# An attention routine that keeps its scores negated, and takes fewer small VectorE operations per unit

## The reference

```python
def diff_attention(q, k, v, lam, slopes):
    ...
        s = jnp.einsum('bhcqd,bhckd->bhcqk', qb, k).astype(jnp.float32) * scale
        s = s - slopes[None, :, None, None, None] * dist
        s = jnp.where(dist >= 0, s, -jnp.inf)
        p = jax.nn.softmax(s, axis=-1)
        p = p[:, :, 0] - lam * p[:, :, 1]
        return jnp.einsum('bhqk,bhkd->bhqd', p.astype(v.dtype), v)

def selected_attention(q, k, v, sel_idx, slopes):
    ...
        s = s - slopes[None, :, :, None, None] * dist
        s = jnp.where(dist >= 0, s, -jnp.inf)
        p = jax.nn.softmax(s, axis=-1)
        return jnp.einsum('bhgqk,bhqkd->bhgqd', p.astype(vg.dtype), vg)
```

## Time and profile before

| What | Value |
|---|---|
| Median of 3 runs | 2819.24 us (2817.35 to 2819.33) |
| The profiled execution, its own time | 2822.95 us |
| Its span in the trace | 2820.8 us |
| PE busy in the span | 2575.7 us, 91% |
| DVE busy in the span | 1466.9 us, 52% |
| ACT busy in the span | 1013.2 us, 36% |
| The three attention calls | 516 to 816 us and 848 to 992 us of the span |

### The profile page before, as it was taken

How to read it: one execution, slowest core, us unless ns; L and a number is a source line. 1 busy time by engine, 2 the same in 40 slices (tenths; PEclk the granted TensorE clock), 3 DMA queues, 4 the chain that set the end, 5 groups by cost and what they waited for, 6 DMA issues and landing times. The chain is left out here.

```text
span 2820.8 us, 34813 instructions
## 1 busy us (share of the span) xinstructions
PE 2575.7 (91%) x12876; PEld 2119.4 (75%) x12876; DVE 1466.9 (52%) x3370; ACT 1013.2 (36%) x2275; POOL 180.5 (6%) x188
## 2 busy tenths in 40 slices
PE   8999986899996679997989999889799999999998
PEld 6887865777985668885658888666578887888877
DVE  5244266855888874218874732478672323223235
ACT  4223132444674442217861232344442223122132
POOL 2000000000000011101200001343000000000000
PEclk9999986799998989999999999899799999999999
DMA  4112120000000054110011132000541111111113
GB/s 149 31 46 78 56 62 1 1 1 1 1 1 1 1 175 116 38 27 14 25 53 49 49 131 101 30 1 1 194 157 38 49 55 47 49 49 46 49 55 143
DMA packets 105079, 153.05 MB, mean 54 GB/s; under 512 B 35408, under 2 KB 49872, under 8 KB 104912
## 3 DMA queue, kind: packets, MB, share of 16 engines
q1 hardware_dynamic: 96464, 125.67, 14.1%
q0 software_dynamic: 3840, 12.59, 1.1%
q10 hardware_dynamic: 4608, 12.58, 1.1%
HBM read 121.44 MB, written 29.36 MB: 53 GB/s over the span
## 5 line engine op out<-in xcount | busy, mean ns | idle before, releaser
L202 PE MATMUL banks<-mhT,mmwhi 128*128 128x512 f32 x1024 | 316.1, 390 | 3.9 <-ACT qsq L2925 2.8
L193 PE MATMUL banks<-mmwhi,fT 128*128 128x512 f32 x1024 | 315.6, 390 | 3.7 <-ACT qsq L2925 3.7
L193 PE MATMUL banks<-g1whi,hT 128*128 128x512 f32 (+1 forms) x1024 | 304.8, 381 | 7.9 <-ACT gates L428 2.9
L177 DVE TENSOR_TENSOR mmwlo<-mmwraw,mmwhi 128x512 fp32r<-128x512 f32 x144 | 97.1, 689 | 368.8 <-ACT mmwhi L172 368.8
L172 ACT ACTIVATE mmwhi<-mmwraw 128x512 fp32r<-128x512 f32 x144 | 89.3, 629 | 412.6 <-DMA mmwraw<-in_w_down 206.6
L193 PEld LDWEIGHTS banks<-mmwhi,fT 128*128 128x128 f32 x1024 | 191.8, 188 | 45.1 <-ACT qsq L2925 5.4
L202 PEld LDWEIGHTS banks<-mhT,mmwhi 128*128 128x128 f32 x1024 | 191.6, 188 | 45.4 <-ACT qsq L2925 4.1
L193 PEld LDWEIGHTS banks<-g1whi,hT 128*128 128x128 f32 x1024 | 188.7, 189 | 45.9 <-issue 4.4
L202 PE MATMUL banks<-mhT,mmwlo 128*128 128x512 f32 x512 | 199.3, 389 | 0.0
L193 PE MATMUL banks<-mmwlo,fT 128*128 128x512 f32 x512 | 199.3, 389 | 0.0
L193 PE MATMUL banks<-g1wlo,hT 128*128 128x512 f32 (+1 forms) x512 | 194.2, 379 | 0.0
(11 more groups left out here) (443 smaller groups left out, 5444.0 us busy)
## 6 DMA issues: line engine op xcount, KB each, us to landing
mmwraw<-in_w_up SPq DMA_DIRECT2D x64, 256.0 KB, 2.7
mmwraw<-in_w_down SPq DMA_DIRECT2D x64, 256.0 KB, 2.6
g1wraw<-in_w_in SPq DMA_DIRECT2D x56, 256.0 KB, 2.7
g3wraw<-in_w_in SPq DMA_DIRECT2D x40, 256.0 KB, 2.6
qx<-x_scratch SPq DMA_DIRECT2D x16, 512.0 KB, 6.8
xt<-in_x SPq DMA_DIRECT2D x8, 512.0 KB, 5.1
z_scratch<-zst POOLq DMA_DIRECT2D x16, 256.0 KB, 4.1
cw<-in_cmp_w SPq DMA_DIRECT2D x2, 2048.0 KB, 10.0
```

Of the source, the lines that this page charges most:

```text
L177: self.nc.vector.tensor_tensor(self.lo[n][:, c], self.raw[n][:, c], f32(self.hi[n][:, c]), ALU.subtract)\
L193: ins = self.nc.tensor.matmul(out, l, r[:, c], start=k == 0 and i == 0, stop=k == self.nk[j] - 1 and i == 2)
L202: ins = self.nc.tensor.matmul(out, l[:, col], r, start=k == 0 and i == 0, stop=k == self.nk[j] - 1 and i == 2)
```

## The change

In `bias_max` the scale becomes negative, the start value 3e38 and the reduction a minimum, so that the SBUF tile holds the negated scores and the accumulator gives the negated maximum itself. The separate negation is gone, and the link between the two with it; `m_ready` is now incremented by the accumulator's readout. The exponential has scale -1. The statistics tile is laid out with the map as the last index, so that the two sums of a unit lie side by side: `weights` takes one reciprocal of two columns, and forms the factor with one scalar_tensor_tensor in place of two products. The optional sink logit, which no call uses, is removed along with its semaphore.

```diff
-    st = mem.at(f"{name}st", stat_kb, [P, 16, 8], F32)
+    st = mem.at(f"{name}st", stat_kb, [P, 8, 16], F32)
...
                     nc.scalar.activation(x[s % XR][:, 0:un.n], x[s % XR][:, 0:un.n], ACT.Exp,
-                                         bias=st[:, s % 16, 1:2],
-                                         accum_out=st[:, s % 16, 2:3]).then_inc(e_ready, 1)
...
+                                         bias=st[:, 1, s % 16:s % 16 + 1], scale=-1.0,
+                                         accum_out=st[:, 2, s % 16:s % 16 + 1]).then_inc(e_ready, 1)
...
-                ch.link(nc.vector.tensor_tensor_reduce(out=x[s % XR][:, 0:un.n], in0=score_bank(s),
-                                                       in1=un.table, scale=un.scale,
-                                                       scalar=-3e38 if un.sink is None else un.sink, op0=ALU.add,
-                                                       op1=ALU.max, accum_out=st[:, s % 16, 0:1]))
-                nc.vector.tensor_scalar(st[:, s % 16, 1:2], st[:, s % 16, 0:1], -1.0, None,
-                                        ALU.mult).then_inc(m_ready, 1)
+                nc.vector.tensor_tensor_reduce(out=x[s % XR][:, 0:un.n], in0=score_bank(s), in1=un.table,
+                                               scale=-un.scale, scalar=3e38, op0=ALU.add, op1=ALU.min,
+                                               accum_out=st[:, 1, s % 16:s % 16 + 1]).then_inc(m_ready, 1)
...
-                ch.link(nc.vector.reciprocal(st[:, a, 3:4], st[:, a, 2:3]))
+                ch.link(nc.vector.reciprocal(st[:, 3, a:a + maps], st[:, 2, a:a + maps]))
                 if maps == 2:
-
-                    ch.link(nc.vector.reciprocal(st[:, b, 3:4], st[:, b, 2:3]))
-                    ch.link(nc.vector.tensor_tensor(st[:, b, 4:5], st[:, a, 2:3], st[:, b, 3:4], ALU.mult))
-                    ch.link(nc.vector.tensor_tensor(st[:, b, 5:6], st[:, b, 4:5], C["nlam"][:], ALU.mult))
+                    ch.link(nc.vector.scalar_tensor_tensor(out=st[:, 5, b:b + 1], in0=st[:, 2, a:a + 1],
+                                                           scalar=C["nlam"][:], in1=st[:, 3, b:b + 1], op0=ALU.mult,
+                                                           op1=ALU.mult))
```

More of the change, by code:

```diff
@@ L1095, in __init__ @@
     def __init__(self, t, q, k_hi, k_lo, k0, table, scale, v, dv, sel, coef, out, add,
-                 k1=None, sink=None, out_free=None, out_col=0):
-        self.sink, self.out_free = sink, out_free
+                 k1=None, out_free=None, out_col=0):
+        self.out_free = out_free
         self.out_col = out_col
@@ L1116, in attention_stage @@
     o_ready, o_done, chain = sem(name + "_o"), sem(name + "_od"), sem(name + "_chain")
-    sink_ready = sem(name + "_sink")
     chunks, c_end = [], []
@@ L1265, in weights @@
                 dve.wait_ge(e_ready, s + maps)
-                if un.sink is not None:
-                    dve.wait_ge(sink_ready, u + 1)
-                    ch.link(nc.vector.tensor_tensor(st[:, a, 2:3], st[:, a, 2:3], st[:, a, 6:7], ALU.add))
-                ch.link(nc.vector.reciprocal(st[:, a, 3:4], st[:, a, 2:3]))
+                ch.link(nc.vector.reciprocal(st[:, 3, a:a + maps], st[:, 2, a:a + maps]))
                 if maps == 2:
-                    ch.link(nc.vector.reciprocal(st[:, b, 3:4], st[:, b, 2:3]))
-                    ch.link(nc.vector.tensor_tensor(st[:, b, 4:5], st[:, a, 2:3], st[:, b, 3:4], ALU.mult))
-                    ch.link(nc.vector.tensor_tensor(st[:, b, 5:6], st[:, b, 4:5], C["nlam"][:], ALU.mult))
+                    ch.link(nc.vector.scalar_tensor_tensor(out=st[:, 5, b:b + 1], in0=st[:, 2, a:a + 1],
+                                                           scalar=C["nlam"][:], in1=st[:, 3, b:b + 1], op0=ALU.mult,
+                                                           op1=ALU.mult))
                     nc.vector.scalar_tensor_tensor(out=x[a % XR][:, 0:un.n], in0=x[b % XR][:, 0:un.n],
-                                                   scalar=st[:, b, 5:6], in1=x[a % XR][:, 0:un.n], op0=ALU.mult,
+                                                   scalar=st[:, 5, b:b + 1], in1=x[a % XR][:, 0:un.n], op0=ALU.mult,
                                                    op1=ALU.add).then_inc(p_ready, 1)
                 elif un.coef is not None:
-                    ch.link(nc.vector.tensor_tensor(st[:, a, 3:4], st[:, a, 3:4], un.coef, ALU.mult))
+                    ch.link(nc.vector.tensor_tensor(st[:, 3, a:a + 1], st[:, 3, a:a + 1], un.coef, ALU.mult))
             def output(u):
@@ L1288, in output @@
                 if un.add:
-                    nc.vector.scalar_tensor_tensor(out=un.out, in0=ps, scalar=st[:, a, 3:4], in1=un.out,
+                    nc.vector.scalar_tensor_tensor(out=un.out, in0=ps, scalar=st[:, 3, a:a + 1], in1=un.out,
                                                    op0=ALU.mult, op1=ALU.add).then_inc(o_done, 1)
                 else:
-                    nc.vector.tensor_scalar(un.out, ps, st[:, a, 3:4], None, ALU.mult).then_inc(o_done, 1)
+                    nc.vector.tensor_scalar(un.out, ps, st[:, 3, a:a + 1], None, ALU.mult).then_inc(o_done, 1)
             for s in issue[0]:
```

3 lines of the change are left out of this document (removed).

## The result

The changed kernel takes 2793.12 us (median of 4 runs, 2788.87 to 2796.18), against 2819.26 us before: 26.1 us less, ratio 0.9904 with an interval of 0.9892 to 0.9916. The forecast was 2792.0 us. In two later sets on other occasions the same kernel took 2788.93 and 2791.37 us, at ratios 0.9888 and 0.9899, which is 28 to 32 us less than the kernel before in those sets. One execution of the kernel before in the last of these sets took 5173 us, in a slow state, and no ratio counts it.

The account below looks back on a forecast made before the run. PE was taken to bound the one-map stages, and a loop through other engines the two-map stage. 12.5 + 10.9 - 1.0 + 4.4 + 0.4 = 27.2 us off 2819.2 gave 2792.0 us, range 2785 to 2800.

Parts of the forecast that it names:

- The bound: PE bounds the two one-map stages; in the two-map stage a loop through other engines sets the pace.
- The tail: Two-map stage, reciprocal to combination: four links of 0.195 become two, 0.39 a unit, 12.5 us over 32 units.
- The negation: Two-map stage: without the negation and its link the second exponential starts earlier, mean 0.34 a unit, 10.9 us.
- The formula: Two-map second exponential's start after the first pass; r is pass to readout, e the exponential's length; gain 0.38 at width 768.
- The clock: Two-map stage: TensorE's low clock, assumed until 872 us, slows two units of width 384; 1.0 us off, bounds 0 and 2.
- The one-map stages: PE's waits at small widths shrink by 0.17 each, 26 times, 4.4 us; earlier first exponentials add 0.4 us.
- The sum: All terms together: 12.5 + 10.9 - 1.0 + 4.4 + 0.4 = 27.2 us, giving 2792.0 us.
- The dearer minimum: Rival: in the score passes the minimum costs 0.06 us more than the maximum; gain 21 to 22, 2797.5 us; chance 0.15.
- The larger share of the one-map stages: Rival: all 10.2 us of PE's waits in the one-map stages come back, 2786 us; chance 0.12.
- The readout does release ScalarE sooner: Rival claimed it does not: only the tail and the second pass's link gain, about 15 us, 2804; chance 0.04.
- The low clock that holds on: Rival: PE's low clock lasts longer in the two-map stage; through width 896 some 14 us slower, 2833; chance 0.02.

Follow-up runs that it names:

- e4: Changed kernel with the change in the two-map stage alone; the one-map stages keep the maximum and its negation: 2796.68 us, ratio 0.9917 to the kernel before.
- e2: Kernel before with only the new statistics layout and new tail (one two-column reciprocal, one factor operation), maximum and negation kept: 2810.08 us, ratio 0.9964.
- e3: Kernel before with the two reciprocals made one of two columns; both products and the negation stay: 2813.23 us, ratio 0.9969.
- e5: Changed kernel, but the pass reads its start value 3e38 from an SBUF column instead of a constant: 2796.52 us, ratio 0.9911 to the kernel before.
- e1: Changed kernel with the old tail of two reciprocals and two products, so the negated scores alone: 2801.38 us, ratio 0.9938 to the kernel before.
- e6: Changed kernel with one unlinked small VectorE operation put back behind each pass: 2795.46 us, ratio 0.9911 to the kernel before.
- e9: Changed kernel with only VectorE's wait for each pass's own readout put back, no operation added: 2798.05 us, ratio 0.9922 to the kernel before.
- e8: The changed kernel unaltered, timed again as reference in a later set: 2788.93 us, ratio 0.9888 to the kernel before.
- e11: The changed kernel unaltered, timed a third time as reference in another set: 2791.37 us, ratio 0.9899 to the kernel before.
- e7: Changed kernel with the maps' order swapped, so 1 / sum 2 and its product with -lambda form during the last exponential: 2786.18 us, ratio 0.9874 to the kernel before.
- e10: As e7, with an earlier unit's output moved between the prepared product and the last one: 2785.47 us, ratio 0.9877 to the kernel before.

## Why the prediction was right, step by step

**The bound.** The two-map stage was a loop through VectorE and ScalarE in which PE waits, and the one-map stages were PE's. Both were read rightly. The units of the two-map stage give 21.5 us, in the changed kernel and in e4 alike, and what e4 lacks to the whole change, 7 us in its trace and 4 to 8 in the medians, is the part of the one-map stages.

**The tail.** "They are four links of 0.195 and become two" was mis-sized: 12.5 us forecast, 10.5 measured (e2). The pitch of the two-column reciprocal is 0.20, as forecast (e3); the factor operation, which reads lambda from a column, has 0.26. A hint stood in the earlier trace rows, where 0.06 was put down to the minimum as the possible price of a rival, while e5 shows that it belongs to the scalar from a column. That the 0.06 of the factor operation is the same price is likely, but no run shows it apart from the kind of operation.

**The negation.** 10.9 us forecast. The formula (2r + 0.56 before; the larger of r + e + 0.11 and 2r + 0.14 after) gives the start of the second exponential. For widths 128, 768 and 1024 it has 0.98, 2.30 and 2.84 before, measured 0.94, 2.30 and 2.84, and 0.72, 1.92 and 2.42 after, measured 0.73, 1.93 and 2.41. e1 alone has the unit of width 768 at 4.695 for 4.70, and 11.0 us over all units for 10.9. e6 and e9 show why: the readout's release of ScalarE and the lost link carry the gain, the operation itself next to nothing. The sentence of the Trainium skill ("VectorE: DVE Perf Modes", "The DRAIN you can't avoid") that the next operation waits until the pipeline is empty, weighed in the prediction at 0.5 us, lost against the row: the second pass starts with the readout (906.13). The same section goes on to say that a next operation that is not held starts earlier, which the prediction left out and which this trace agrees with.

**The clock.** The 1.0 us taken off did not come. TensorE's clock was up at 862 us and not, as was assumed, at 872. Counted from the first pass that is 19 us in place of 23, with PE busy 11.8 of 14 us where it had been 13.6 of 20. Units of width 256, which ran at 1.2 GHz, gained 0.613, and the formula with the measured tail has 0.28 + 0.33. That the denser work brought the clock up sooner is not shown: three traces of the changed kernel have the first low stretch of the stage 17, 14 and 7 us long (changed, e8, e11), so much of its length changes from one execution to the next. Here it made no difference, as the unit times are the same in all three.

**The one-map stages.** 4.8 us forecast, 6.7 in the profile (2.6 and 4.1), 6.9 over three traces. The waits of the weight loads fell by 2.9 us only. Much of the rest lies where the clock changes: units of width 256 in "wi" went from 1.50 to 1.27 us, more than the 0.17 of a negation, with the clock up 11 us behind the first pass in place of 18. What they gain goes with how long the clock stays low: with it up after 14 to 15 us they take 1.39 and 1.37 (e8, e11), and in e1, where it came up after 17 us, 1.45. Why it comes up sooner in the faster kernels is not shown. Units of width 384 and 512 in "wi", at 2.4 GHz, gain 0.12 and 0.07 each time.

**The sum.** The misses cancel: -2.0 in the tail, +0.1 in the negation, +1.0 for the clock, +1.9 in the one-map stages, which makes 28.2 in the attention stages. In the profiled pair the transposes between "wi" and "di" are 1.3 us shorter, the start of "sl" 1.4 later and all that follows "di" 1.3 longer, with no edit in any of them: 26.8 us of span. The mechanism was forecast and came; that the median lies only 1.1 us off the forecast is luck, since the same kernel's medians lie 4 us apart.

**The rivals.** The dearer minimum is out (553 ns, e5). The larger share of the one-map stages was half right in size, though not by its mechanism: 7.3 of the 10.2 us of waits are still there. The readout does release ScalarE sooner (0.11). The low clock that holds on did not come: by 862 us TensorE was at 2.4 GHz.

## What to carry to other kernels

In a loop between two engines, write the start of each step as a sum of pitches and take the larger of the two engines' forms: after the change it gave the start of the second exponential to 0.01 us here, and told that ScalarE, not VectorE, caps what the freed time is worth. A small operation that nothing waits for is nearly free beside a long one (0.06 and less); what costs is a link (0.12) and every step between the last input and the instruction that the other engine waits for. So move what is known early, here 1 / sum 2 and its product with lambda, into the idle time before the last input: e7 took another 0.19 us out of units of width 768 and 896, and 4.9 us out of all 32.

## What the runs showed of the hardware that was not expected

- A start value that VectorE's pass reads from a column in place of a constant costs 0.06 us an instruction (e5): 613 against 553 ns at width 384, 1013 against 951 at width 768.
- Behind a pass with a readout, the next instruction starts with the readout (906.13 for both in the changed kernel) where nothing waits, and 0.12 later where it waits for that readout's semaphore (e9).
- An instruction of VectorE that has two semaphores to wait for started 0.29 us after ScalarE's readout (e7), one with a single wait 0.21 to 0.22 (e10 and the changed kernel).
- TensorE was granted 1.2 GHz at the head of each of the three stages, and for the same kernel the time differs from trace to trace: 17, 14 and 7 us at the head of "di" in the changed kernel, 20 before. In some traces it was granted 1.2 GHz once more, for about 3 us, at the end of "di".
